# Reordering the work around the expert dispatch of a hybrid attention and mixture-of-experts step

## The reference, cut to what matters

```python
    x = x + gt1 * mixed                      # mixed = (...) @ w_out
    h2 = rms_norm(x, g_norm2) * (1 + sc2) + sh2
    x = x + gt2 * moe(h2, w_router, b_router, w_gate, w_up, w_down)
# moe: scores = sigmoid(h2 @ w_router); best group of experts, then the top 2 in it;
#      out += combine[e] * (silu(h2 @ w_gate[e]) * (h2 @ w_up[e])) @ w_down[e]
```

## Time and profile before

| | us |
|---|---|
| median of 3 runs | 1833.3 (1832.22 to 1834.5) |
| the profiled execution, its own time | 1832.64 |
| its span, first to last instruction | 1830.9 |
| PE busy in it | 1658.5 (91%) |
| DVE busy | 1052.5 (57%) |
| ACT busy | 812.7 (44%) |
| mean granted TensorE clock | 0.954 of 2.4 GHz |

### The profile page before, as it was taken

One profiled execution on the slowest core, in us unless ns is written; L12 is line 12 of the kernel. 1 busy time (PEld: TensorE's weight loads), 2 busy tenths in 40 slices (PEclk: granted clock), 3 DMA queues, 4 the chain that ended last, 5 costly groups with the idle time before them and its releaser, 6 DMA issues. The chain is left out here.

```text
span 1830.9 us, 21965 instructions
## 1 busy us (share of the span) xinstructions
PE 1658.5 (91%) x8224; PEld 1221.0 (67%) x8224; DVE 1052.5 (57%) x1827; ACT 812.7 (44%) x1473; POOL 227.9 (12%) x284
## 2 busy tenths in 40 slices
PE   3899999999998789999969999999999986999990
PEld 0677777777776556767536777777778774776660
DVE  2567655346554666666476666444656556676644
ACT  2344553355322336565453445344552323565641
POOL 1001000011000022222020000001110001222212
PEclk8999999999999799999989999999999987999995
DMA  9342225434644599999747202453444536999975
GB/s 352 112 171 69 70 77 177 144 113 148 235 147 188 206 359 412 413 413 413 305 164 249 93 27 67 153 192 105 156 150 138 207 127 262 408 413 412 413 296 195
DMA packets 107034, 400.41 MB, mean 219 GB/s; under 512 B 12736, under 2 KB 12768, under 8 KB 106416
## 3 DMA queue, kind: packets, MB, share of 16 engines
q1 hardware_dynamic: 73152, 266.37, 38.8%
q0 software_dynamic: 33632, 130.01, 19.5%
q10 hardware_dynamic: 144, 2.62, 0.4%
HBM read 348.03 MB, written 49.45 MB: 217 GB/s over the span
## 5 line engine op out<-in xcount | busy, mean ns | idle before, releaser
L1701 PE MATMUL ps<-hi,hT_hi 128*128 128x512 f32 x960 | 396.1, 413 | 17.9 <-DVE lo L1107 8.8
L1107 DVE TENSOR_TENSOR lo<-raw,hi 128x1024 fp32r<-128x1024 f32 x298 | 353.0, 1221 | 97.6 <-ACT hi L768 94.9
L1703 PE MATMUL ps<-hi,hT_lo 128*128 128x512 f32 x960 | 379.0, 395 | 0.0
L1702 PE MATMUL ps<-lo,hT_hi 128*128 128x512 f32 x960 | 378.4, 394 | 0.0
L768 ACT ACTIVATE hi<-raw 128x1024 fp32r<-128x1024 f32 x298 | 300.4, 1056 | 147.2 <-DMA raw<-w_stream 139.3
L1701 PEld LDWEIGHTS ps<-hi,hT_hi 128*128 128x128 f32 x960 | 183.4, 191 | 79.9 <-issue 21.2
L1703 PEld LDWEIGHTS ps<-hi,hT_lo 128*128 128x128 f32 x960 | 182.5, 190 | 41.0
L1702 PEld LDWEIGHTS ps<-lo,hT_hi 128*128 128x128 f32 x960 | 183.8, 191 | 33.2
L2038 PE MATMUL ps<-over,xT 128*128 128x512 f32 x288 | 127.7, 595 | 1.7 <-DMA over<-w_moe 1.2
L1701 PE MATMUL ps<-hi,xT_hi 128*128 128x512 f32 x256 | 104.4, 408 | 3.7 <-DVE xT_lo L1576 3.7
L1702 PE MATMUL ps<-lo,xT_hi 128*128 128x512 f32 x256 | 101.4, 396 | 0.0
(11 more groups left out here) (279 smaller groups left out, 2690.1 us busy)
## 6 DMA issues: line engine op xcount, KB each, us to landing
raw<-w_moe SPq DMA_DIRECT2D x192, 512.0 KB, 11.7
raw<-w_stream SPq DMA_DIRECT2D x112, 512.0 KB, 3.5
over<-w_moe SPq DMA_DIRECT2D x108, 512.0 KB, 13.3
raw_m<-w_stream SPq DMA_DIRECT2D x70, 512.0 KB, 5.7
ye_d<-ysb POOLq DMA_DIRECT2D x50, 512.0 KB, 7.1
bias_na<-na_bias POOLq DMA_DIRECT2D x32, 384.0 KB, 3.3
sg<-sg_d POOLq DMA_DIRECT2D x8, 1280.0 KB, 9.3
raw_p<-w_stream SPq DMA_DIRECT2D x16, 512.0 KB, 17.2
```

The source lines that it names most:

```text
L1107: dve.tensor_tensor(lo[s][:], raw[s][:], hi[s][:].bitcast(F32), ALU.subtract).then_inc(is_lo.sem, 1)
L1701: pe.matmul(out, w_hi, m_hi, start=first, stop=False)
L1702: pe.matmul(out, w_hi, m_lo, start=False, stop=False)
L1703: return pe.matmul(out, w_lo, m_hi, start=False, stop=last)
```

## The change

It reorders instructions; none is added or taken out.

1. DVE: the five `ahead` splits of `w_out` go ahead of the waits for `x` and the gate, and `norm_gain()` goes behind the five `residual(0, t)`.
2. DVE: `inverse_root(1, t)` and `mid_modulate(t)` follow `mid_mean(t)` of the same tile, no longer one tile later.
3. PE: behind tile t of `w_out`'s right half come `router(t - 2)` and `h2_transposes(t - 1)`, one tile sooner than before.
4. ACT: `mid_evac(t - 1)` instead of `mid_evac(t - 2)`, and the Tanh table load stands behind `mid_evac(3)`.
5. SP: expert 1's units 4 and 5 are loaded behind `head_pair(5)`, its units 1 and 2 behind a new wait for the last normed tile, both ahead of `head_pair(6)`; units 0 and 3 stay behind over 0.
6. ACT and DVE: the splits of the next layer's units 0 to 2 go behind the work of expert tile 24.

```diff
@@ SP
-                for p in range(5, KC):
+                head_pair(5)
+                weights(base_at[1], 4, MU)
+                sp.wait_ge(h_ready.sem, h_ready.at(l, 2 * NT - 1))
+                weights(base_at[1], 1, 3)
+                for p in range(6, KC):
                     head_pair(p)
...
                 over_weights(0)
-                weights(base_at[1], 0, MU)
+                weights(base_at[1], 0, 1)
+                weights(base_at[1], 3, 4)
@@ ACT
                     if t < 2:
                         moe_hi(0, 2 + t)
-                    else:
-                        if t == NT - 1:
-                            act.activation(dummy[:, 0:1], dummy[:, 1:2], ACT.Tanh)
-                        mid_evac(t - 2)
-                mid_evac(NT - 2)
+                    if t >= 1:
+                        mid_evac(t - 1)
+                act.activation(dummy[:, 0:1], dummy[:, 1:2], ACT.Tanh)
                 mid_evac(NT - 1)
@@ ACT, expert loop: moved from ahead of the silu to the end of the tile
                     if after is None and l + 1 < DEPTH:
                         for w in range(3):
                             next_hi(w)
@@ DVE
                 m_lo(NT - 1)
+                for u in range(FIRST[("w_out", 0)], NU):
+                    ahead(u)
                 dve.wait_ge(x_back.sem, x_back.at(l, 0))
                 dve.wait_ge(gate_loaded.sem, gate_loaded.at(l, 1))
-                norm_gain()
-                for u in range(FIRST[("w_out", 0)], NU):
-                    ahead(u)
...
                 for t in range(NT):
                     residual(0, t)
+                norm_gain()
...
                 for t in range(NT):
                     residual(1, t)
-                    if t >= 1:
-                        inverse_root(1, t - 1)
-                        mid_modulate(t - 1)
                     mid_mean(t)
-                inverse_root(1, NT - 1)
-                mid_modulate(NT - 1)
+                    inverse_root(1, t)
+                    mid_modulate(t)
@@ DVE, expert loop: next_lo(0..2) moved in the same way as next_hi
@@ PE
                 def w_out_behind(t):
                     if t >= 2:
-                        h2_transposes(t - 2)
-                    if t >= 3:
-                        router(t - 3)
+                        router(t - 2)
+                    if t >= 1:
+                        h2_transposes(t - 1)
...
                 project_by_tile(("w_out", 1), hT_hi, hT_lo, w_out_behind)
-                h2_transposes(NT - 2)
                 head_pair(2)
-                router(NT - 3)
                 router(NT - 2)
                 h2_transposes(NT - 1)
                 router(NT - 1)
```

More of the change, by code:

```diff
@@ L1050, in _ @@
                             moe_hi(after, k)
-                    if after is None and l + 1 < DEPTH:
-                        for w in range(3):
-                            next_hi(w)
                     act.wait_ge(*unit_used(l, n, 3))
@@ L1066, in _ @@
                         moe_hi(n, 5)
+                    if after is None and l + 1 < DEPTH:
+                        for w in range(3):
+                            next_hi(w)
                 ys(MOE_TILES - 1)
@@ L1602, in _ @@
                             moe_lo(nxt, k)
-                    if nxt is None and l + 1 < DEPTH:
-                        for w in range(3):
-                            next_lo(w)
                     dve.wait_ge(silu_done.sem, silu_done.at(l, n))
@@ L1619, in _ @@
                         moe_lo(n, 5)
+                    if nxt is None and l + 1 < DEPTH:
+                        for w in range(3):
+                            next_lo(w)
                 ys(MOE_TILES - 1)
```

## The result

| | before | after |
|---|---|---|
| median of 4 runs, us | 1832.76 (1829.64 to 1834.5) | 1804.02 (1801.83 to 1804.55) |
| profiled execution, its span, us | 1830.9 | 1802.7 |
| mean granted clock of 2.4 GHz | 0.954 | 0.961 |

The ratio is 0.9843 (0.9826 to 0.986), 28.7 us less in the medians against the 33.3 forecast. The profiled execution of after took 1804.55 us.

A forecast was written before the change was run, and what follows sets the result against it. Expert stages were taken as bound by PE and DMA together, the dispatch by a chain from `w_out` to the scores. Terms 15.5 + 6.5 + 4.0 + 2.0 + 5.0 = 33.0 us off 1832.6 gave 1799.6, predicted 1800 us, bounds 1794 to 1812.

The forecast's parts named there:

- Front of `w_out`: Splits ahead of the late vector end PE's 7.77 us wait; right half starts 9.7 us sooner in layer 1, 1.0 in layer 2.
- The loop without lag: In `w_out`'s right half DVE limits at tile 1 only: new PE wait of 1.3 us in layer 1, 0.9 in layer 2.
- The tail: From tile 4's sum to the scores less work is left; scores come 15.5 us sooner in layer 1, 6.5 in layer 2.
- Between S and X: From the scores to the first expert tile: a chain of DVE's small operations, which nothing in the change alters.
- Cover: SP's new loads (2 MB, about 5 us) come ahead of head pairs 6 and 7: cost zero, bounds 0 to 3 us.
- Rival (a): Preloaded units delay head pairs 6 and 7 or the last row store; layer 1 loses 5 to 10 us; chance 0.09.
- Start of the experts 4.0 us: Layer 1, expert tile 1: four early units remove waits of 1.87 and 0.75 us and 1.4 lost to low clock.
- Starvation of the second layer 2.0 us: Layer 2's expert stage: a 5 us DMA head start covers 2.3 us of starvation over six periods; bounds 0 to 2.3.
- Rival (b): DMA paces the expert stage, which keeps its end: the 4.0 and 2.0 go, up to 3 more per layer; chance 0.07.
- End of layer 1: At tile 24, moving silu and `hid` ahead removes a 3.60 us wait and 2.8 of low clock: 5.0 us (2.5 to 5.5).
- Rival (c): Tile 1's new wait drops the clock in the right-half loop: 48 us lost, 1848; chance 0.04 with any other loss.
- Rival (d): An unseen DVE wait leaves only the front and end waits counting: 9.7 + 5 gives 1818; chance 0.05 with mixtures.

The follow-up runs named there:

- e8: The changed kernel with part 5 undone (expert 1's six units all loaded behind over 0, as before): 1806.76 us, ratio 0.9843.
- e5: The changed kernel with expert 1's units 0 and 3 loaded ahead of over 0: 1802.99 us, ratio 0.9831.
- e1: The kernel before with part 1 alone (splits ahead of the waits, norm_gain behind the five residuals): 1820.19 us, ratio 0.9932.
- e3: The kernel before with part 5 alone (four of expert 1's six units loaded ahead of head pair 6): 1832.41 us, ratio 0.9998.
- e10: The changed kernel with the sixth unit of over tiles 1 to 8 not loaded in each layer: 1798.32 us, ratio 0.9808.
- e4: The kernel before with part 6 alone (next layer's splits behind the work of expert tile 24): 1828.2 us, ratio 0.9972.
- e2: The kernel before with parts 2 to 4 alone (norm without lag, transposes, routers and copies one tile sooner): 1823.28 us, ratio 0.9944.
- e11: The changed kernel with norm_gain put back ahead of the five left-half residuals, but behind the splits: 1804.44 us, ratio 0.9837.
- e6: The changed kernel with nine extra 256-column matmuls on PE ahead of layer 2's first row transposes: 1800.91 us, ratio 0.9811.

## Why the prediction was right, and where it was not

- **Front of `w_out`**, right. PE's wait is gone, the right half begins 30.6 us behind W1 where the prediction had 30.8. Part 1 alone gave 10.1 us (9.7 forecast).
- **The loop without lag**, right. New wait at tile 0's transposes 0.91 and 1.13 us (1.3 and 0.9 forecast), none at tiles 1 to 3. Tile 4's sum is read 65.4 and 63.2 us behind W; the forecast, from its 603.0 and 1490.1, was 65.9 and 63.2.
- **The tail**, right in size: 15.0 of 15.5 us, 6.9 of 6.5. For the first layer I took a value between the clocks; PE ran all of it from tile 4's transposes on at the low one, 12.3 us from tile 4's sum to S, where the low end of the prediction had 12.2. That tile 4's sum came 0.5 us earlier than forecast made up for part of it. In the second layer the wait of 1.06 us ahead of router 3 (1.3 forecast) was followed by low clock from tile 4's transposes on, but router 3 itself ran in 1.96, so the fall that the low end had put at that wait came one step later. The value of 1502.9 was a choice between two clocks, and the 1502.5 that came (W2 to S2 from the old W2) is near it by that choice.
- **Between S and X**, right: 16.83 and 16.90 us. Cover: 0 of 0 to 3. Over 0 was issued 16.8 us behind S, at 630.27 (near 631). Rival (a) did not happen.
- **"Start of the experts 4.0 us"** is a term that was mis-sized: 2.4 in the pair of profiles, some 1.5 over all (e8). Of the 4.0, 1.4 were the low clock behind tile 1, and that part came (granted clock 1.00 from 652 to 660 us, 0.82 in the same place before). The other 2.6 were the two waits, and the assumed step, that four early units take away both, failed: 1.05 and 0.76 us are left, since ACT splits in order and stands 5.45 us for unit 0, which is issued last, behind over 0. With unit 0 issued first (e5) ACT's wait goes, but the stage gets no shorter. The term also took the clock of the first expert tile as given; between profiles it makes a difference of 1.6 us, though not between before and after.
- **"Starvation of the second layer 2.0 us"** failed: the six periods took 182.12 us where 180.6 were forecast, and part 5 gives nothing from X2 on. The term rested on one profile, in which six periods took 182.9 us. The five profiles without the early loads have 180.3 to 182.9 there (mean 181.4, and 180.26 in e1), the eight with them and all bytes 180.6 to 182.8 (mean 181.6): a steady 2.3 us to be won was not there, only scatter of that size. Nor did the head start of 5 us, counted on for DMA, show: in e3, where the stage begins no sooner, it gives nothing from X2 on either (303.25 against 303.03). Why it doesn't is open.
- **Rival (b)** happened in a small form: the 4.0 shrank and the 2.0 went, but nothing was lost besides. In e10, with load taken away, no wait for over weights is left.
- **End of layer 1**, right: 5.6 of 5.0 us (5.1 in e4), the last matmuls take 3.68 us (3.6 forecast).
- **Rival (c)**, low clock in the loop, did not happen: granted clock 0.96 from 538 to 614 us. **Rival (d)** did not either: the loop's part (e2) gave 6.5 and 5.1 us.
- The lower bound of 1794 leaves out the 0.7 us that the forecast adds for the median; with it the bound is 1795.

The parts that carry the result (front, loop, tail, end of layer 1) were forecast at 27.0 us together and gave 27.5. The 33.0 us forecast and 28.2 found differ by the two terms on the expert stage (6.0 forecast, 1.9 in the pair of profiles) and by 1 us of scatter in stretches that the change leaves alone.

## What to carry to other kernels

On an engine that works in order, look for work whose input is long there but that stands behind a wait for something late (here splits behind a vector's load: 10 us). Price a change ahead of a stage as a shift of one moment. The expert stages here, with PE and DMA both full, kept nearly all of such a shift and gave almost nothing for loads moved ahead of them. And a wait or a period of 1 or 2 us that one profile shows is no term of a sum until a second profile shows it too: here six periods of the second layer differed by up to 2.6 us among kernels with the same order of loads.

## What the runs showed of the hardware

- The length of a wait alone does not tell what clock follows. A wait of 1.88 us behind nearly unbroken matmuls was followed by transposes of 1.70 us (e11), one of 1.84 us behind 5.6 us of 256-column matmuls by transposes of 1.10 us (e6; over the whole first tile behind it the granted clock was 0.84), waits of 0.91 and 1.13 us by full speed. One wait of 1.57 us, in the first expert tile of the first layer, stands in all fourteen profiles; seven ran that tile at a granted clock of 1.00 behind it, seven at 0.86.
- Small waits in the tail of the dispatch, 0.48 and 0.69 us among transposes and 16-column router matmuls, went with the low clock (1.88 and 3.59 us). Four added 256-column matmuls brought 1.04 and 1.96 in the first layer; in the second the transposes took 1.33 for 1.93, and the last router stayed slow at 3.59 (granted clock 0.56 from 1471.9 to 1477.6).
- The rows gathered for the first tile arrive 1.8 us sooner in the second layer if the over loads are held back until then (S to X 16.80 against 18.58 us).
